# Attention scores by pairs of heads: three float32r products in turn from two partition halves, and a decay that TensorE adds

## The reference

```python
qa, ka, va, fa, qb, kb, vb, qc, kc, vc, g = split(x @ w_in)           # head_dim 64
ya = fox(qa, ka, va, fa + b_f)       # 6 heads, causal, with decay
yb = dilated(rope(qb), rope(kb), vb) # 4 key heads, 3 query groups (128,1) (512,4) (2048,16)
yc = moba(rope(qc), rope(kc), vc)    # 6 heads; at 256 positions plain causal attention
merged = gates[0]*(ya @ w_pa) + gates[1]*(yb @ w_pb) + gates[2]*(yc @ w_pc)
x = layer_norm(ALPHA * x + merged @ w_o)
x = layer_norm(ALPHA * x + (silu(x @ w_gate) * (x @ w_up)) @ w_down)

def fox(q, k, v, f_logit):
    c = cumsum(log_sigmoid(f_logit))                    # per head, along the positions
    logits = q @ k.T * scale + c[query] - c[key]        # the decay; then causal mask
    return softmax(logits) @ v
```

## Time and profile before

| | |
|---|---|
| three runs | 905.82, 906.30, 906.94 us, median 906.3 |
| span of the profiled execution | 905.5 us |
| TensorE matmuls busy | 869.5 us (96%) |
| VectorE busy | 534.9 us (59%) |
| ScalarE busy | 396.6 us (44%) |
| GpSimd busy | 52.0 us (6%) |
| DMA, 16 engines | 50.2% of the span |

### The profile page before, as it was taken

The page is one execution under the profiler, slowest core; times in us unless marked ns, Lnnn a source line. Parts: engine busy times, 40 slices in busy tenths (PEclk is TensorE's granted clock), DMA queues, the critical chain, the costliest instruction groups (busy, mean ns, idle before and its releaser), DMA issues.

```text
span 905.5 us, 10788 instructions
## 1 busy us (share of the span) xinstructions
PE 869.5 (96%) x4148; PEld 711.6 (79%) x4148; DVE 534.9 (59%) x814; ACT 396.6 (44%) x541; POOL 52.0 (6%) x100
## 2 busy tenths in 40 slices
PE   2999999999998999999999999999999899999995
PEld 1887787788887888888878788877888788888884
DVE  6575564646787545445685656555658855445436
ACT  3463445545434434444337444554543454344330
POOL 0011142000000000000000213300000000000000
PEclk9999999999999999999999999999999999999998
DMA  8572424256544855565436342333664575665601
GB/s 305 171 266 82 140 74 137 93 186 223 183 150 170 274 188 184 188 194 176 152 106 232 118 139 82 128 117 117 209 232 140 175 247 189 211 196 161 215 1 47
DMA packets 93314, 149.34 MB, mean 165 GB/s; under 512 B 3408, under 2 KB 52688, under 8 KB 93264
## 3 DMA queue, kind: packets, MB, share of 16 engines
q1 hardware_dynamic: 93264, 148.65, 50.2%
HBM read 147.59 MB, written 1.05 MB: 164 GB/s over the span
## 4 chain that ended last, share of the span: by engine, by line
PE 85%; DVE 7%; ACT 3%; DMA 2%; issue 2%; POOL 1%; SPq 0%; DVEq 0%; POOLq 0%
PE bank L1016 74%; PE bank L1079 4%; DVE w_lo L827 3%; PE bank L1031 2%; DMA raw<-in_w_in 2%; PE bank L1101 2%; ACT w_hi L745 1%; PE bank L1091 1%; PE bank L1041 1%; DVE stats L950 1%; DVE x L983 1%; DVE x L947 1%; DVE x L980 1%; DVE act_lo L832 0%; PE bank L1059 0%
## 5 line engine op out<-in xcount | busy, mean ns | idle before, releaser
L827 DVE TENSOR_TENSOR w_lo<-raw,w_hi 128x2048 fp32r<-128x2048 f32 (+3 forms) x142 | 307.4, 2168 | 93.6 <-ACT w_hi L745 93.3
L1016 PE MATMUL bank<-w_hi,act_hi 128*128 128x512 f32 (+2 forms) x864 | 343.0, 397 | 3.4 <-DVE act_lo L832 3.4
L1016 PE MATMUL bank<-w_hi,act_lo 128*128 128x512 f32 (+2 forms) x864 | 332.9, 385 | 0.0
L1016 PE MATMUL bank<-w_lo,act_hi 128*128 128x512 f32 (+2 forms) x864 | 332.2, 384 | 0.0
L745 ACT CAST w_hi<-raw 128x2048 fp32r<-128x2048 f32 (+3 forms) x142 | 257.1, 1812 | 131.6 <-PE bank L1016 102.1
L1016 PEld LDWEIGHTS bank<-w_hi,act_hi 128*128 128x128 f32 x864 | 162.8, 188 | 38.5 <-DVE act_lo L832 3.8
L1016 PEld LDWEIGHTS bank<-w_hi,act_lo 128*128 128x128 f32 x864 | 162.7, 188 | 33.0
L1016 PEld LDWEIGHTS bank<-w_lo,act_hi 128*128 128x128 f32 x864 | 163.2, 189 | 28.6
L1016 PE MATMUL bank<-w_hi,y_hi 128*128 128x512 f32 x240 | 95.2, 396 | 0.0
L1016 PE MATMUL bank<-w_hi,y_lo 128*128 128x512 f32 x240 | 93.6, 390 | 0.0
L1016 PE MATMUL bank<-w_lo,y_hi 128*128 128x512 f32 x240 | 93.5, 389 | 0.0
(11 more groups left out here) (86 smaller groups left out, 548.8 us busy)
## 6 DMA issues: line engine op xcount, KB each, us to landing
raw<-in_w_in SPq DMA_DIRECT2D x48, 1024.0 KB, 5.1
raw<-in_w_gate SPq DMA_DIRECT2D x44, 512.0 KB, 3.9
raw<-in_w_up SPq DMA_DIRECT2D x44, 512.0 KB, 4.9
raw<-in_w_down SPq DMA_DIRECT2D x22, 1024.0 KB, 4.9
raw<-in_w_o SPq DMA_DIRECT2D x8, 1024.0 KB, 5.0
raw<-in_w_in SPq DMA_DIRECT2D x4, 768.0 KB, 4.4
raw<-in_w_pa SPq DMA_DIRECT2D x4, 768.0 KB, 4.4
raw<-in_w_pc SPq DMA_DIRECT2D x4, 768.0 KB, 4.4
```

The lines of the kernel that those rows point to most:

```text
L827: dve.tensor_tensor(weights(w_lo, i, HI_SLOTS), weights(raw, i, RAW_SLOTS), weights(w_hi, i, HI_SLOTS).bitcast(F32), ALU.subtract).then_in ...
L1016: ins = pe.matmul(bank[use[0]][:, 0:width], a, w[:, k, c0:c0 + width], start=start and k == 0 and p == 0, stop=stop and k == nk - 1 and p ...
```

## The change

A unit is now a pair of heads and a tile of positions: 16 units a layer where there were 32. `tick` plans `turn_p` of unit k-2 and the scores of unit k; a new `half_tick`, in the next `attend`, plans the values of unit k-2 and, for dilated units with t=1, the third group's scores (`scores2`). So a unit takes two blocks.

The scores are three float32r products (hi·hi, hi·lo, lo·hi) of queries and keys; the instructions of the two heads stand in turn, one from partitions 0 to 63 into bank 4, the next from 64 to 127 into bank 5. `turn_qk` is followed by a ScalarE rounding to `qk_hi` and a VectorE subtraction to `qk_lo`, instead of one VectorE copy.

The forgetting heads get their decay as a fourth product: `forget_sum` is one block of four float32r matmuls that leaves the running sums of every head in rows; ScalarE and VectorE store them in `cum_row` as hi and lo rows; a matmul with a 0/1 column `pick` adds the head's row to the scores. The term `c[query]` is the same along a row and falls out of the softmax. The mask is the causal table for all heads. TensorE waits for `cum_row` before forgetting scores.

Both heads of a unit share `turn_p` (one bank, one ScalarE copy, half as many) and `values` (one bank, one reciprocal of 2 columns, one multiply). The counts of transposes and of value matmuls stay.

```diff
+        units = [(b, p, t) for b in range(3) for p in range(PAIRS[b]) for t in range(TT)]
...
+        def half_tick():
+            k = tick_at[0] - 1
+            if 0 <= k < len(units) and stage_of[k]["b"] == 1 and stage_of[k]["t"]:
+                stage_of[k]["s2"] = [bank(4), bank(5)]
+                plan.append(("scores2", stage_of[k], g0 + 1))
+            if 0 <= k - 2 < len(units):
+                d = stage_of[k - 2]
+                d["o"] = aux_bank()
+                plan.append(("values", d, g0 + d["b"]))
...
-            if ticks and tick_at[0] < len(units) + 3:
+            if ticks and mid[0]:
+                half_tick()
+                mid[0] = False
+            elif ticks and tick_at[0] < len(units) + 2:
                 tick()
+                mid[0] = True
...
-                        plan.append(("decay", layer, 0, aux_bank()))
...
+                elif kind == "turn_qk":
+                    act.wait_ge(filled[b], n)
+                    act.copy(qk_hi[ev["g"] % 2][:, ev["pair"]:ev["pair"] + ev["np"], ev["t"] * P:(ev["t"] + 1) * P],
+                             group_view(bank[b], ev["np"], P)).then_inc(qk_hi_done, 1)
+                elif kind == "forget_sum":
+                    act.copy(cum_row[:, :], bank[b][:, 0:SEQ]).then_inc(cum_hi_done, 1)
...
+                    dve.wait_ge(cum_hi_done, layer + 1)
+                    for r in (32, 96):
+                        ins = dve.tensor_tensor(cum_row[r:r + 32, :], bank[b][r:r + 32, 0:SEQ],
+                                                cum_row[r:r + 32, :].bitcast(F32), ALU.subtract)
+                    ins.then_inc(drained[b], 1)
...
+                    if br == 0:
+                        cb, cn = cum_use[step[3]]
+                        pe.wait_ge(drained[cb], cn)
...
+                    for gi in groups:
+                        for p, (a, k) in enumerate(((qk_hi, qk_hi), (qk_hi, qk_lo), (qk_lo, qk_hi))):
+                            for e, (b, n) in enumerate(uses):
+                                rows = slice(e * HEAD_DIM, (e + 1) * HEAD_DIM)
+                                ins = pe.matmul(bank[b][:, off:off + w], a[g % 2][rows, q, t * P:(t + 1) * P],
+                                                k[g % 2][rows, K_PAIR[br] + pair, 0:w], start=p == 0,
+                                                stop=p == 2 and br > 0)
+                    if br == 0:
+                        for e, (b, n) in enumerate(uses):
+                            pe.matmul(bank[b][:, 0:w], pick[rows, h:h + 1].broadcast_to([HEAD_DIM, P]),
+                                      cum_row[rows, 0:w], start=False, stop=True).then_inc(filled[b], 1)
```

More of the change, by code:

```diff
@@ L62 @@
 HI_SLOTS, RAW_SLOTS = 5, 3
+PAIRS = [h // 2 for h in BRANCH_HEADS]
 HELD = 3
-STAGES, PSLOTS = 2, 3
+STAGES = 2
 FFN_CHUNKS = D_FF // 256
@@ L536, in trunk @@
         tables = sb("tables", [P, TABLE_COLS])
[L537 to L540, removed]
+        cum_row = sb("cum_row", [P, SEQ], F32R)
+        pick = sb("pick", [P, FOX_HEADS], F32R)
+        neg_max = sb("neg_max", [P, 8])
+        denom = sb("denom", [P, 8])
+        rdenom = sb("rdenom", [P, 8])
         f_bias = sb("f_bias", [P, DEPTH, FOX_HEADS])
@@ L691, in link @@
                 pool.wait_ge(pool_own, own)
-            pool.wait_ge(tables_loaded, 32)
+            for part in (logf_hi, logf_lo):
+                pool.memset(part[:, :, :].bitcast(F32), 0.0).then_inc(logf_zeroed, 1)
+            pool.wait_ge(tables_loaded, 48)
             for step in PLAN:
@@ L1046, in _ @@
                     _, layer, use = step
+                    cum_use[layer] = use
                     pe.wait_ge(logf_lo_done, layer + 1)
                     out, done = take(use)
[L1049 to L1057 removed]
@@ L1064, in _ @@
                     ins.then_inc(done, 1)
-                elif kind == "scores":
-                    _, u, g = step
-                    br, h, t, w = u["b"], u["h"], u["t"], u["w"]
+                elif kind in ("scores", "scores2"):
+                    u, g = step[1], step[2]
+                    br, pair, t, w = u["b"], u["p"], u["t"], u["w"]
                     qb, qn = u["qk"]
                     pe.wait_ge(drained[qb], qn)
-                    at = (h % 2) * HEAD_DIM
-                    keys = qk_t[g % 2][at:at + HEAD_DIM, K_PAIR[br] + h // 2, 0:w]
-                    for gi in range(GROUPS if br == 1 else 1):
-                        q = h + gi * DIL_KV_HEADS
-                        use = u["s"][1] if gi == 2 and t else u["s"][0]
-                        if gi == 0 or (gi == 2 and t):
-                            take(use)
-                            off = 0
-                        queries = qk_t[g % 2][at:at + HEAD_DIM, q // 2, t * P:(t + 1) * P]
-                        ins = pe.matmul(bank[use[0]][:, off:off + w], queries, keys, start=True, stop=True)
-                        off += w
-                        if br != 1 or gi == 2 or (gi == 1 and t):
-                            ins.then_inc(filled[use[0]], 1)
@@ new lines, in _ @@
+                    uses = u["s"] if kind == "scores" else u["s2"]
+                    if br == 0:
+                        cb, cn = cum_use[step[3]]
+                        pe.wait_ge(drained[cb], cn)
+                    for use in uses:
+                        take(use)
+                    groups = [0]
+                    if br == 1:
+                        groups = [2] if kind == "scores2" else [0, 1] if t else [0, 1, 2]
+                    for gi in groups:
+                        off = 0 if kind == "scores2" else gi * w
+                        q = pair + gi * PAIRS[1]
+                        for p, (a, k) in enumerate(((qk_hi, qk_hi), (qk_hi, qk_lo), (qk_lo, qk_hi))):
[4 more added lines that the diff above has]
+                                                stop=p == 2 and br > 0)
+                                if br and p == 2 and gi == groups[-1]:
+                                    ins.then_inc(filled[b], 1)
```

225 lines of the change are left out of this document (110 added, 115 removed).

## The result

The changed kernel takes **889.46 us** (median of 4 runs, 888.94 to 891.06) against 906.06 us (905.54 to 906.94) for the kernel before on the same chip: ratio 0.9819 [0.9805, 0.9833]. The forecast was 891. The profiled execution took 889.12 us and has a span of 887.3.

The account below looks back on a forecast made before the run. TensorE, issuing without pause in attention, was taken as the bound: 905.5 − 27.9 (queue) + 2.7 (sums wait) + 10.0 (`stage` waits) = 890.3 us, 891 with 0.8 from span to median; range 883 to 911, likeliest case 887 to 896.

Parts of the forecast that it names:

- Price of a pair, 0.06 an instruction: TensorE's attention scores: two array halves run at once, so 312 instructions cost 0.06 us each, 18.7 us; chance 0.42.
- the ends (0.06 and 0.116): Score instruction prices in us: halves at once, scores gain 22.0 us; halves one behind the other, 4.5 us.
- one behind the other: Rival on the scores: array halves do not overlap, each instruction costs about 0.116 us, 908 to 909 us; chance 0.31.
- a drain for each change of half: Rival on the scores: each switch between array halves costs 0.165 us, 51 us for 312, about 957 us; chance 0.08.
- Taking in turn: Score instructions alternating between the two heads' halves; the serial rival said this buys nothing.
- Visits and decays, −9.2 (21.1 to 11.9) and −5.9: TensorE's entries into 64-partition scores fall from 64 to 36 at 0.33 us; decays and small products removed gain 5.9 us.
- Wait on the sums, +2.7: Before the first forgetting scores TensorE waits for `cum_row` behind VectorE's `w_lo`: 1.3 us, in two layers 2.7.
- Waits on `stage`, 11.7 in 8, longest 1.8: TensorE waits for GpSimd's rotated queries at pieces 3 to 6: 5.85 us a layer; net +10.0 after 1.7 existing.
- The extra ScalarE rounding of queries and keys hides too: Rounding queries and keys for float32r scores costs nothing, since what it feeds is read blocks later.
- −27.9 (queue): TensorE's queue in attention shrinks by 22.0 us from scores and visits plus 5.9 from decays.
- Forecast −15.2: Total change: 27.9 us less queue, 2.7 more for the sums, 10.0 more for `stage`.
- the waits on `stage` do not come: Rival: halves run at once and the new waits stay hidden, 877 to 880 us; chance 0.13.

Follow-up runs that it names:

- Experiment 1: Changed kernel with all three score passes of the first head before those of the second, instead of in turn: 889.65 us, ratio 0.9817.
- Experiment 2: Changed kernel with plain float32 scores, still in pairs, queries and keys copied once by VectorE without rounding: 886.64 us, ratio 0.9785.
- experiments 4 and 6: 4: changed kernel, `cum_row` written before the weight remainder, 890.5 us. 6: plain float32 pairs with copy first, 879.2; sums first too, 880.16; later turn instead, 878.99; with sums, 878.01.
- experiment 5: Changed kernel with the turn of the last forgetting queries and keys planned one block earlier: 888.4 us, ratio 0.9803.
- experiments 3 and 6: 3: changed kernel, rotated turn one `attend` later, 881.56 us, or copy to `stage` before the exponentials, 880.87. 6: plain float32 pairs, copy first and sums first, 880.16.

## Why the prediction held, step by step

- **Price of a pair, 0.06 an instruction: right.** Pairs are 0.11 to 0.12 us apart. 156 pairs at 0.114 and 36 visits at 0.34 are 30.0 us; forecast 30.6. The choice between the ends (0.06 and 0.116) decided the case, and no row bore on it. The rivals "one behind the other" and "a drain for each change of half" fall by the same rows. (The drain's 957 was added to the time of before; with the forecast's own other terms it is 942 to 960. Nothing hangs on it.) The Trainium skill (TensorEngine Tiling (Array Packing), Key Properties) says that tiles of one mode load weights and multiply in parallel; the trace agrees, with two of each in 0.11 us.
- **"Taking in turn"**: the forecast tied the overlap to it in name only, its arithmetic to the two halves. Experiment 1 shows that the order buys nothing. Experiment 2 shows that neither do the three passes: without them the kernel is 2.8 us faster.
- **Visits and decays, −9.2 (21.1 to 11.9) and −5.9: right as far as they can be read.** The visit is 0.34 by the row above. No run took the visits, the pairs and the decays apart; TensorE's busy time as a whole fell by 27.3 us (869.5 to 842.2), against 27.9 for the three.
- **Wait on the sums, +2.7: 2.8.** As worked out: TensorE is there at 59.4 (forecast 59.5) and waits 1.39 us (1.3). Its price in time was less: experiments 4 and 6 show that with it gone some, most or more of it turns up elsewhere.
- **Waits on `stage`, 11.7 in 8, longest 1.8: 10.4 in 8, longest 1.9.** +8.7 instead of +10.0. The mechanism is shown at piece 6, in the timeline of the changed kernel:

```profile
110.59 2.29 DVE L856 TENSOR_TENSOR w_lo<-raw,w_hi 128x2048 fp32r<-128x2048 f32 x1
...
112.15 1.03 POOL L723 TENSOR_TENSOR rope_cos<-stage,tables 128x128 f32<-128x128 f32 x1 [12.12 <-ACT stage L781]
...
114.56 0.42 PEld L1065 LDWEIGHTS bank<-tables,stage 128*128 128x128 f32 x4 [1.75 <-POOL stage L726]
```

  Block at 109.52, `stage` ready 5.0 us behind it, a wait of 1.75: the forecast had 5.05 and 1.8. Pieces 3 and 4 of layer 0 have 1.88 and 1.26 (forecast 1.75 and 1.3). What was too large was piece 5, 0.29 against 1.0: its rounding rest is narrower (1.75 us instead of 2.29) and ends at 95.82, when the rotation has just begun (95.53):

```profile
94.07 1.75 DVE L856 TENSOR_TENSOR w_lo<-raw,w_hi 128x1536 fp32r<-128x1536 f32 x1
...
97.11 0.20 PEld L1065 LDWEIGHTS bank<-tables,stage 128*128 128x128 f32 x2 [0.29 <-POOL stage L726]
```

- **"The extra ScalarE rounding of queries and keys hides too": wrong.** It is the step of the forecast that failed. What it feeds is read late, but VectorE's queue behind it is not: the wait on the log-forgets grew by 2.5 us (0.8 to 3.3). Experiment 2, which has no rounding, takes 2.4 of it away, experiment 5 1.3.
- **Waits of before that went with their cause, 2.3 us (`y_lo`, `prob_t`): missed.** Argued only; no run was made on them.
- **The balance.** −27.9 (queue) + 2.8 + 8.7 + 2.5 − 2.3 = −16.2, against −16.6 in the medians. Forecast −15.2. The measured sum mixes rows of PEld and PE; with those of PE alone (+8.0 and +2.4 in place of 8.7 and 2.5) it is −17.0, so it is good to about half a us. The sums on the page of the profile close: busy time −27.3, idle time +9.1 (36.0 to 45.1), together the −18.2 of the spans, of which 1.4 are the start. That the total came within 1.5 us is in part luck: the two misses, +2.5 and −2.3, nearly cancel.

The rival "the waits on `stage` do not come" had 877 to 880. The two experiments that take only them away have 881.56 and 880.87, a little above, since the other new waits stay; with the plain float32 scores as well, two of the four kernels also with the sums first, it is 878.0 to 880.2.

## What to carry to other kernels

Matmuls of 64 partitions cost half (here 0.11 to 0.12 us for two instructions instead of for one) when the upper and lower half of the array have work in the same visit: bring both heads into one visit and keep visits few. The order inside, with three of a half in a row, changed nothing, and plain float32 in place of the three float32r passes was 2.8 us faster. When TensorE gains time ahead of a chain through other engines, look for the turn that now comes too early and read the length of the chain from the trace; here 8 of 28 us gained were lost so, and moving one step, of TensorE or of the copy, gave them back. An instruction that "hides" on an engine still has a place in its queue: ask what stands ahead of it and waits for a DMA.

## What the runs showed of the hardware that was not expected

- Matmuls of two array halves overlap even when three instructions of one half stand in the program ahead of those of the other (experiment 1: 889.65 against 889.46 us): in the records the first of the upper half starts 0.010 us behind the first of the lower, ahead of the lower half's second and third. Their weight loads, too: two in 0.11 us.
- Plain float32 products on two halves overlap as float32r does, with two of a half in a row: twelve instructions in 0.86 us (experiment 2).
- A GpSimd step of 0.32 or 0.45 us that is caught by a VectorE instruction with two SBUF inputs lasts 2.25 to 2.57 us, until 0.2 to 0.3 us behind it, though the step before it was free (experiments 3 and 6).
